# Three changes of order in the attention loops of a two-block transformer kernel: convolution taken apart over the turns, raw gates copied one tile at a time, the next product's first unit laid into the last turns of the causal loop

## What is computed

```python
# first block
att_a = dsa_branch(...)     # 8 heads, one shared key head; each query keeps its top 128 keys; softmax
att_b = fox_branch(...)     # 8 heads, causal softmax with a decay added to the logits
m_a, m_b = split(sigmoid(h @ w_merge), 2)
out = (m_a * ((att_a * silu(gate_a)) @ w_branch_a) + m_b * ((att_b * silu(gate_b)) @ w_branch_b)) @ w_out
# second block, layer 0 (even): 8 heads of differential attention, two softmax maps each,
# x queries see 256 + 512 keys, context queries 256
out_a = rms_norm(diff_attend(q, k, v, lam)) * silu(ga)
out_b = b * conv3(c * u) * silu(gb)         # depthwise convolution over tokens, 3 taps, width 512
# second block, layer 1 (odd): 8 heads of neighbourhood attention (256 near keys + 256 context keys)
out_x = concat(neighbourhood(q, k, v) * silu(gn), fourier_mix(ud) * silu(gd)) @ w_out
```

## Time and profile before

| | us |
|---|---|
| median of three runs | 1272.52 (1270.68 to 1272.96) |
| the profiled execution's own time | 1269.73 |
| its span, first to last instruction | 1267.9 |
| busy: PE / PEld / DVE / ACT / POOL | 1225.8 / 990.5 / 676.3 / 631.4 / 463.6 |
| of the chain that ended last: PE / DVE / ACT | 76% / 11% / 8% |
| PE idle by the profile, whole span | 42 |
| of it in the causal, even and near loop (windows 200:340, 628:829, 1080:1176) | 6.7 / 4.9 / 3.2 |

### The profile page before, as it was taken

The page is one execution under the profiler, slowest core; times in us unless marked ns, Lnnn a source line. Parts: engine busy times, 40 slices in busy tenths (PEclk is TensorE's granted clock), DMA queues, the critical chain, the costliest instruction groups (busy, mean ns, idle before and its releaser), DMA issues.

```text
span 1267.9 us, 19561 instructions
## 1 busy us (share of the span) xinstructions
PE 1225.8 (97%) x7148; PEld 990.5 (78%) x7148; DVE 676.3 (53%) x1294; ACT 631.4 (50%) x1342; POOL 463.6 (37%) x360
## 2 busy tenths in 40 slices
PE   7999999999999999999999999999999999999997
PEld 5877777677788878888878887787878788777686
DVE  4576975766414354647475766713825600655353
ACT  6544325655522355923366666635445522755543
POOL 5544353222343635621332333231352224232351
PEclk9999999999999999999999999999999999999999
DMA  6331542000422523240435322311263321321443
GB/s 235 109 108 67 188 149 96 35 35 34 150 100 87 215 98 125 75 150 3 148 128 197 135 90 100 101 42 60 100 216 131 113 106 67 100 68 67 167 122 111
DMA packets 28573, 140.33 MB, mean 111 GB/s; under 512 B 4320, under 2 KB 5728, under 8 KB 16000
## 3 DMA queue, kind: packets, MB, share of 16 engines
q1 hardware_dynamic: 21728, 117.72, 26.6%
q10 hardware_dynamic: 6752, 21.35, 5.1%
HBM read 122.74 MB, written 6.29 MB: 102 GB/s over the span
## 4 chain that ended last, share of the span: by engine, by line
PE 76%; DVE 11%; ACT 8%; issue 3%; DMA 1%; POOL 1%; DVEq 0%; ACTq 0%; POOLq 0%; SPq 0%
PE psum L663 46%; PE psum L691 6%; PE psum L801 4%; DVE arena L2345 2%; PE psum L1072 2%; DVE small L2342 2%; PE psum L1048 2%; PE psum L843 2%; PE psum L1056 2%; PE psum L651 2%; PE psum L940 2%; PE psum L1211 1%; ACT w_high L1443 1%; DMA w_raw<-stream 1%; PE psum L1179 1%
## 5 line engine op out<-in xcount | busy, mean ns | idle before, releaser
L1255 POOL TENSOR_TENSOR w_low<-w_raw,w_high 128x512 fp32r<-128x512 f32 x256 | 350.0, 1380 | 636.4 <-ACT w_high L1443 635.9
L1443 ACT CAST w_high<-w_raw 128x512 fp32r<-128x512 f32 x256 | 153.8, 623 | 253.4 <-PE psum L663 166.6
L663 PE MATMUL psum<-x_high,w_high 128*128 128x512 f32 x528 | 219.0, 415 | 7.1 <-ACT merge_a L1657 2.0
L663 PE MATMUL psum<-x_high,w_low 128*128 128x512 f32 x528 | 206.5, 391 | 0.0
L663 PE MATMUL psum<-x_low,w_high 128*128 128x512 f32 x528 | 206.2, 391 | 0.0
L663 PEld LDWEIGHTS psum<-x_high,w_high 128*128 128x128 f32 x528 | 99.6, 189 | 37.1 <-issue 12.8
L663 PEld LDWEIGHTS psum<-x_high,w_low 128*128 128x128 f32 x528 | 99.1, 188 | 21.6
L663 PEld LDWEIGHTS psum<-x_low,w_high 128*128 128x128 f32 x528 | 99.6, 189 | 16.6 <-issue 1.0
L663 PE MATMUL psum<-w_high,x_high 128*128 128x512 f32 x224 | 88.4, 395 | 0.8 <-POOL w_low L1255 0.6
L2555 DVE TENSOR_REDUCE small<-psum 128x1 f32<-128x768 f32 (+1 forms) x96 | 69.9, 769 | 32.9 <-PE psum L1048 32.8
L663 PE MATMUL psum<-w_high,x_low 128*128 128x512 f32 x224 | 87.3, 390 | 0.0
(11 more groups left out here) (480 smaller groups left out, 2798.4 us busy)
## 6 DMA issues: line engine op xcount, KB each, us to landing
w_raw<-stream SPq DMA_DIRECT2D x97, 1024.0 KB, 4.9
x_kept<-arena ACTq DMA_DIRECT2D x8, 512.0 KB, 4.2
arena<-x_kept ACTq DMA_DIRECT2D x8, 512.0 KB, 6.3
arena<-bias ACTq DMA_DIRECT2D x8, 512.0 KB, 4.1
q_masked<-e_q_high SPq DMA_DIRECT2D x24, 96.0 KB, 2.5
arena<-x SPq DMA_DIRECT2D x4, 512.0 KB, 5.2
arena<-x ACTq DMA_DIRECT2D x4, 512.0 KB, 5.0
arena<-ctx ACTq DMA_DIRECT2D x4, 512.0 KB, 5.4
```

Source lines behind the costliest of these rows:

```text
L663: mm = pe.matmul(o, l, r, start=(first and n == 0 and kind != "fc"), stop=(last and n == len(passes) - 1))
L1255: pool.tensor_tensor(PLACE[u][1], RAW[:, g % 2, u % 4, :], PLACE[u][0].bitcast(F32), ALU.subtract).then_inc(w_lo, 1)
L1443: act.copy(PLACE[u][0], RAW[:, g % 2, u % 4, :]).then_inc(w_hi, 1)
```

## The change

The kernel after does the same arithmetic. The convolution becomes a generator of pieces: multiply, first tap, second tap, third tap, each its own piece, two pieces a turn, with semaphore `conv_tap` in place of `link`. The narrow accumulators are copied by ACT one by one, each in the turn after it closed. The four tiles of unit 0 of `mb0` are taken in turns 64 to 67 of the causal loop. In the near loop ACT's turn gets another order.

```diff
@@ PE, tiles() @@
                     if last:
                         fills_bank(mm, key)
+                        if chunk in NARROW:
+                            closed.append(key)
@@ PE, gemm() @@
-            def gemm(chunk, x, c=None, ready=None, midway=None, part="xc"):
+            def gemm(chunk, x, c=None, ready=None, midway=None, part="xc", first=0):
-                for k in range(n):
+                for k in range(first, n):
@@ PE, causal loop @@
                 if s < len(BOTH):
                     feed("ab", pieces, 1)
+                if s == len(BOTH):
+                    pool[0], turn[ALL] = ALL, 7
+                    pieces = tiles("mb0", 0, X)
+                if s >= len(BOTH):
+                    next(pieces, None)
                 if s >= 8 and s % 4 == 0:
                     values_both(s // 2 - 3)
...
-            pool[0], turn[ALL] = ALL, 7
-            gemm("mb0", X)
+            gemm("mb0", X, first=1)
@@ ACT, causal loop @@
-            def kept_raw(c):
-                for j in range(2):
-                    key = (f"ma{c}", j)
-                    ps = filled(act, key)
-                    frees(act.copy(MA[:, 2 * c + j, :], ps[:, :]), key)
+            def kept_raw(c, j):
+                ps = filled(act, (c, j))
+                frees(act.copy(MA[:, 2 * int(c[2]) + j, :], ps[:, :]), (c, j))
             for s in range(len(BOTH) + 5):
-                for c in range(4):
-                    if ended[f"ma{c}"] == ("ab", s - 1):
-                        kept_raw(c)
+                for key, at_step in closed_at.items():
+                    if at_step == ("ab", s - 1):
+                        kept_raw(*key)
@@ ACT, near loop (gates_raw is changed as kept_raw is) @@
             for s in range(steps + 6):
-                for c in ("gn0", "gn1", "gd0", "gd1"):
-                    if s and ended[c] == ("n", s - 1):
-                        gates_raw(c)
+                if s >= 7 and s % 2:
+                    values_near((s - 7) // 2)
+                for key, at_step in closed_at.items():
+                    if at_step == ("n", s - 1):
+                        gates_raw(*key)
+                if 2 <= s < steps + 2:
+                    turned_near(s - 2)
+                if s < steps:
+                    exps_n(s, ATT["n"].tile(s))
                 if s:
                     high(fed["n"][s - 1] + ROOM)
                 if s < 6:
                     between(s)
-                if 2 <= s < steps + 2:
-                    turned_near(s - 2)
-                if s < steps:
-                    exps_n(s, ATT["n"].tile(s))
-                if s >= 7 and s % 2:
-                    values_near((s - 7) // 2)
                 if s % 8 == 2 and s // 8 < 3:
                     prep_n(s // 8 + 1)
@@ DVE, even loop (convolve and fed_even go) @@
+            def convolution():
+                for key, (phase, f) in closed_at.items():
...
+                    yield f // 2
+                    ps = filled(dve, key)[:, 0:w]
+                    if chunk[:2] == "bb":
...
+                        continue
+                    consumed(dve, (f"cb_{j}", part))
+                    frees(dve.tensor_tensor(z, z, ps, ALU.mult), key)
+                    yield f // 2
+                    consumed(dve, key)
+                    dve.tensor_scalar(y, z, tap(1), None, ALU.mult).then_inc(sig("conv_tap"), 1)
+                    yield f // 2
+                    dve.wait_ge(sig("conv_tap"), 4 * j + 2 * part + 1)
...
+                    yield f // 2
+                    dve.wait_ge(sig("conv_tap"), 4 * j + 2 * part + 2)
...
                 if s:
                     norm_even(s - 1)
-                    fed_even(s - 1)
+                for _ in range(2):
+                    if conv_from < s:
+                        conv_from = next(conv)
```

More of the change, by code:

```diff
@@ L1851, in fed_even @@
             def fed_even(s):
-                for (chunk, part), (_, f) in closed_at.items():
-                    if f // 2 == s and chunk[:2] == "cb":
+                for (chunk, part), (phase, f) in closed_at.items():
+                    if phase == "e" and f // 2 == s and chunk[:2] == "cb":
                         ps = filled(act, (chunk, part))
@@ L2035, in values_near, with gates_raw @@
                 frees(act.copy(N_QT[:, pr, P * t:P * t + P], ps[:, 0:P]), key)
-            def gates_raw(c):
-                for j in range(2):
-                    key = (c, j)
-                    ps = filled(act, key)
-                    frees(act.copy(MA[:, (0 if c[:2] == "gn" else 4) + 2 * int(c[2]) + j, :], ps[:, :]), key)
+            def gates_raw(c, j):
+                ps = filled(act, (c, j))
+                frees(act.copy(MA[:, (0 if c[:2] == "gn" else 4) + 2 * int(c[2]) + j, :], ps[:, :]), (c, j))
             steps = ATT["n"].steps
             for s in range(steps + 6):
-                for c in ("gn0", "gn1", "gd0", "gd1"):
-                    if s and ended[c] == ("n", s - 1):
-                        gates_raw(c)
+                if s >= 7 and s % 2:
[7 more added lines that the diff above has]
+                    exps_n(s, ATT["n"].tile(s))
                 if s:
@@ L2576, in fed_even @@
-            def fed_even(s):
-                for key, (_, f) in closed_at.items():
-                    (chunk, part), j = key, int(key[0][3])
-                    if f // 2 != s or chunk[:2] == "cb":
+            n = len(EVEN)
+            def convolution():
+                for key, (phase, f) in closed_at.items():
+                    chunk, part = key
+                    if phase != "e" or chunk[:2] == "cb":
                         continue
-                    place = slice(S, S + L) if part else slice(0, S)
+                    j, place = int(chunk[3]), slice(S, S + L) if part else slice(0, S)
@@ L2582, in fed_even @@
                     z, y = E_Z[:, place], E_Y[:, j, place]
-                    ps = filled(dve, key)[:, 0:z.shape[-1]]
-                    if chunk[:2] == "ub":
-                        consumed(dve, (f"cb_{j}", part))
-                        frees(dve.tensor_tensor(z, z, ps, ALU.mult), key)
-                        consumed(dve, key)
-                        convolve(j, z, y, z.shape[-1])
-                    else:
+                    w, tap = z.shape[-1], lambda n: col("conv", 4 * n + j)
@@ L2594, in _ @@
+                yield n + 1
+            conv = convolution()
+            conv_from = next(conv)
             for s in range(n + 1):
```

14 lines of the change are left out of this document (7 added, 7 removed).

## The result

The median went to 1260.64 us (five executions, 1260.06 to 1264.72); before, in the same comparison, it was 1270.68. The ratio is 0.9926, interval 0.9905 to 0.9947. The forecast had 1265.4 and a range that ended at 1261.5: the sign was right, the gain larger than said. But the profiled execution of after took 1264.72, with a span of 1262.8 where before had 1267.9: only 5.1 less.

The account below looks back on a forecast made before the run. PE, busy 97% of the 1267.9 us span, was taken as the bound, so only its waits count. 1.7 + 0.3 + 2.7 + 2.4 = 7.1 us takes the median from 1272.5 to 1265.4, range 1261.5 to 1270.0.

Parts of the forecast that it names:

- Part 1: Causal loop, raw gates copied tile by tile: 0.8 in turns 16 and 32, 0.1 in turn 48; 1.7 us.
- Part 2: Unit 0 of `mb0` in the causal loop's run-out: PE 1.7 ahead, then waits 1.4 at `mb1`; 0.3 us left.
- Part 3: Even loop, convolution in pieces: two waits of 1.5 before the scores of turns 9 and 33 go, less 0.3; 2.7 us.
- the rival's mechanism, pieces that delay the maxima: Rival, even loop: each of 16 turns with pieces costs about 1.0; 13 lost against 4.4, 1281 us; chance 0.04.
- collision with POOL: Even loop: a DVE tap beside POOL's low part costs up to 1.0; two on the path leave 0.7 of the gain.
- Part 4: Near loop, ACT's new order and gates tile by tile: values' waits 2.0, bank 6 0.5, less 0.15; 2.4 us.
- bank 6: Near loop, change from `gn0` to `gn1`: PE's wait for this bank, 0.6 start to start, goes; +0.5 us.
- the casts' new place: Near loop: ACT's casts go behind the exponentials, at most 0.7 us later; cover called wide, costed at zero.
- Sum: Whole kernel: 1.7 + 0.3 + 2.7 + 2.4 = 7.1 us saved; as summed, 1263 to 1268, chance 0.60.
- The prediction's tests: Signs: named waits gone, even loop shorter by about 2.7, near loop by about 2.4, new `mb1` wait of 1 to 1.5.
- more than summed: Rival, whole kernel: all upper ends, 10.2 us, give 1262.3, or 1261 with unseen weight-load waits; chance 0.10.
- the saving is the same for both: Last step: profiled execution 1269.7 to 1262.6, 2.8 shorter than the median; same saving takes the median from 1272.5 to 1265.4.

Follow-up runs that it names:

- the second profile of after: Profile from executing the kernel after once more, unchanged; that run measured 1261.38 us, ratio 0.9936 to before.
- the parts alone: Four kernels, each the kernel before with one of the four parts: 1269.42 us, ratio 0.9993, 1267.11 us and 1267.75 us, in order of part.
- the 90: Executions of the unchanged kernel before, made alongside the experiments with each one's mean clock recorded; median 1270.5 us.
- the order alone: Kernel before with only ACT's new order in the near loop, the two gate tiles still copied together; 1.90 us below before, ratio 0.9986.
- the early cast alone: Kernel after with ACT casting the units of ple0 and ple1 one layer-norm tile earlier; median 1261.78 us.
- part 3 alone: Kernel before with only the even loop's convolution in pieces, two a turn; 1267.11 us, ratio 0.9975.
- parts 1, 2 and 4 together: The whole change without the even loop's convolution in pieces; 1263.97 us from six executions, ratio 0.9949.
- the second profile of before: Profile from running the kernel before once more, unchanged, to read each execution's clock; 1270.48 us, ratio 0.9994.

## Why the prediction was right, and where it fell short

- **Part 1** (1.7): measured 1.94 in the whole change and 1.88 alone. Turns 16 and 32 gave 0.81 and 0.79 against 0.8 each, with the wait for DVE's copy next, as forecast:

```profile
224.73 0.88 PE L942 MATMUL psum<-arena 128*64 128x128 f32 x12 [0.31 <-DVE arena L2369]
```

  Turn 48 gave 0.34 in place of 0.1: from the transposes at 282.74 to the tile at 283.33 before took 0.59, after takes 0.24, and of that the idle time shows only 0.1.
- **Part 2** (0.3): 0.26 alone, 0.16 in the whole change (0.36 in the second profile of after). Gain and loss were both smaller than forecast (1.4 against 1.7, 1.2 against 1.4). The new wait at `mb1` came as said, 0.98 by the list.
- **Part 3** (2.7): 2.81, alone 2.69, in the second profile of after 1.70 (see above). The two waits gave 1.57 and 1.55 for 1.5 each. At turns 22 and 23 the lead fell by 0.57 (1.55 to 0.98 at 728.5), where the forecast had 0.3. Not seen was that the same stands at the end of the loop, and dearer: the two short taps of `ub_3` come right before the last maxima, and PE's lead falls by 0.83.

```profile
824.28 0.48 DVE L2595 SCALAR_TENSOR_TENSOR e_conv<-e_conv_in,cols_sb,e_conv 128x255 f32<-128x255 f32 x1
824.79 0.48 DVE L2599 SCALAR_TENSOR_TENSOR e_conv<-e_conv_in,cols_sb,e_conv 128x255 f32<-128x255 f32 x1
825.20 0.16 DVE L2564 RECIPROCAL small<-small 128x2 f32<-128x2 f32 x1
825.27 1.80 DVE L2557 TENSOR_REDUCE small<-psum 128x1 f32<-128x768 f32 x2
```

```profile
828.58 0.63 PE L1062 MATMUL psum<-squares_sb,arena 128*128 128x128 f32 x4 [0.64 <-ACT arena L1847]
```

  That is the rival's mechanism, pieces that delay the maxima, at two places. Together they cost 1.4. It was made up by 0.2 to 0.3 at each of four other places: behind the two waits (667 and 769), where the cause wasn't looked for, and at the modulation rows at 704.7 and 807.2, where PE's wait for the granule is shorter (0.67 and 0.66 in before, 0.43 and 0.47 in after). No collision with POOL was seen on PE's path, but none was looked for piece by piece.
- **Part 4** (2.4): 2.86. The values' waits and bank 6 were as costed. The step that was short is the list of what is late: the transposes at 1090 waited 0.4 for DVE, which waited for ACT's exponential behind the cast. I costed the casts' new place at zero and looked only for a loss in it.
- **Sum** (7.1): 7.8 between the profiles, 7.7 with the parts alone (1.88 + 0.26 + 2.69 + 2.86), 6.9 with the second profile of after, 7.4 to 7.6 between executions at like clock. The prediction's tests came out as said, but for two: the near loop gave 2.86 and not 2.4, and the even loop gave 1.70 in one of the two profiles of after.
- **The rivals.** The measured 1260.64 lies nearest the rival "more than summed" (1262.3, or 1261 with unseen waits of the weight loads). Its mechanism isn't what happened: the parts did not all reach their upper ends (7.8 and not 10.2), and the rest came with the clock and by luck, as the next point says. DVE and ACT are busy 57% to 67% of the three windows, not 54%; nothing hangs on it.
- **The step that failed** is the last: "the saving is the same for both, so the median goes from 1272.5". It took the 2.8 us between the profiled execution and the median for a constant, and a median of three for the level of the kernel. The profiled execution had a mean clock of 0.998. The clock of the one at 1272.52 isn't on record, but all of the 19 among the 90 that took 1272.3 or more had 0.993 or 0.994. So the 2.8 us were for the most part stretches at half clock, which come and go from one execution to the next, and the waits that part 3 removes are among the places where they begin. The median of before was not 1272.5 but 1270.5, once 90 executions are counted; and the gain was 9.3 us (1270.5 to 1261.2; by means 8.8), of which 7.7 at full clock and the remaining 1.6 (by means 1.1) by fewer stretches. In the terms of the prediction: 1270.5 - 7.1 = 1263.4 by its sum, 1262.8 with the right one, 1261.2 with the clock, and the last 0.6 to the measured 1260.64 was luck. The largest of these four errors, 2.0 us, is the level that the forecast started from; the bounds of 1261.5 and 1270.0 hung on the same level.

The clocks bear the last step out. The kernels in which the waits of turns 9 and 33 are open have a mean clock of 0.9956 to 0.9968 (before 0.9960, parts 1, 2 and 4 alone or together, the order alone). Those in which they are gone or filled have 0.9975 to 0.9985, but for one: the early cast alone, 0.9967, with its new wait of 2.1 us. What stays open is how the 1.6 us divides: part 3 alone brought 0.7 beyond its price, parts 1, 2 and 4 together 1.6 beyond theirs (6.59 against 5.0) at a mean clock only slightly higher. The 1.6 is a remainder: it moves with every tenth in the price at full clock, and that price rests on one or two profiles a kernel. With 6 to 12 executions a kernel, and levels 2.2 us apart, that can't be told.

## What to carry to other kernels

Before a forecast is tied to a median of a few executions, read the mean clock of each: where it differs, the level to forecast from is that of one clock, and the others are that plus stretches. A wait of PE of 1.4 to 2.7 us cost its length and, in some executions, another 1.3 to 1.6 us behind it, so its removal can be worth more than the list of waits says, and a wait that only moves keeps that risk. One profile a kernel isn't enough to price a part either: the same part gave 2.8 us in one execution and 1.7 in another. When copies and casts change places on an engine, follow what moves forward as well as what moves back: its gain is as real as the other's loss.

## What the runs showed of the hardware

In every profile each half-clock stretch ahead of the kernel's last few microseconds lies at or behind a wait of PE: at 457 to 460 (idle 2.7), 542.5 (2.3), 660.2 and 760.8 to 764.0 (1.36). The same wait is followed by a stretch in one execution and by none in the next: of the eleven profiles with the wait at 457, eight have a stretch there; of the seven in which the waits of turns 9 and 33 are open, six have one at turn 33 and one has one at turn 9; of all fourteen, which have the wait of 2.3 us at 538 to 544, one. A wait of about the same length as those of turns 9 and 33, at 1010.9 in before (idle 1.28) and in every other profile too, was followed by none. A stretch costs 1.3 to 1.6 us where PE has work: the lead fell by 1.59 at 763 in the second profile of before, and rose by 1.61 at 460 in the profile of part 3 alone, which had none there. Matmuls whose result nobody uses, laid into the waits, kept the clock up: with three waits filled, seven of twelve executions had a mean clock above 0.998, of the kernel before none of 90.
